# Output stage of a two-branch decoder layer on one core: zero fill, weight sums and merged sums moved between engines and places, last store moved from one queue to another

## What is computed

```python
h = rmsnorm(x, norm_g)
proj = einsum('bsd,dc->bsc', h, w_in)          # 1024 x 6656, then split
# branch A: three groups of 4 heads, (window, dilation) = (128,1), (512,4), (2048,16)
y_a = einsum('bsc,cd->bsd', attn_a * silu(z_a), w_pa)
# branch B: 8 heads, blocks of 256 keys; with 512 positions every query sees all its past
y_b = einsum('bsc,cd->bsd', attn_b * silu(z_b), w_pb)
merged = sigmoid(r_a + b_a) * y_a + sigmoid(r_b + b_b) * y_b
x = x + einsum('bsd,de->bse', merged, w_out)
out = rmsnorm(x, final_g)
```

## Time and profile before

| what | value |
|---|---|
| median of 3 runs | 436.65 us (433.98 to 437.82) |
| the profiled execution's own time | 436.65 us |
| its span, first to last instruction | 434.8 us |
| around the span | 1.85 us |
| PE busy | 423.1 us, 97% of the span |
| DVE, ACT, POOL busy | 299.6, 228.3, 218.6 us |
| mean granted clock of PE | 0.992 |

### The profile page before, as it was taken

How to read it: one execution, slowest core, us unless ns; L and a number is a source line. 1 busy time by engine, 2 the same in 40 slices (tenths; PEclk the granted TensorE clock), 3 DMA queues, 4 the chain that set the end, 5 groups by cost and what they waited for, 6 DMA issues and landing times.

```text
span 434.8 us, 7147 instructions
## 1 busy us (share of the span) xinstructions
PE 423.1 (97%) x2557; PEld 376.6 (87%) x2557; DVE 299.6 (69%) x512; ACT 228.3 (53%) x475; POOL 218.6 (50%) x155
## 2 busy tenths in 40 slices
PE   6999999999999999999999999999999999999994
PEld 5789998889889888998888888888999999988883
DVE  3869835265577695766857675495687768589955
ACT  6645555355465676466654565354445544532633
POOL 4854433243274563585559545353435443734890
PEclk9899999999999999999999999999999999999998
DMA  8972244926899879431530217530442144199905
GB/s 286 291 197 99 98 112 132 290 73 243 312 271 338 340 266 296 155 99 28 167 96 0 99 45 283 193 103 31 134 134 77 65 129 133 38 387 405 408 9 194
DMA packets 48835, 76.70 MB, mean 176 GB/s; under 512 B 4360, under 2 KB 39200, under 8 KB 47264
## 3 DMA queue, kind: packets, MB, share of 16 engines
q1 hardware_dynamic: 43904, 67.38, 47.1%
q10 hardware_dynamic: 4896, 8.86, 5.6%
HBM read 55.21 MB, written 14.73 MB: 161 GB/s over the span
## 4 chain that ended last, share of the span: by engine, by line
PE 87%; DMA 6%; DVE 2%; ACT 2%; issue 1%; SPq 0%; DVEq 0%; ACTq 0%
PE ps L1102 14%; PE ps L1103 14%; PE ps L1106 14%; PE ps L1302 5%; PE ps L1301 5%; PE ps L1300 5%; PE ps L1143 4%; PE ps L1145 4%; PE ps L1144 4%; PE ps L1209 3%; PE ps L1190 3%; PE ps L1349 3%; PE ps L1348 3%; PE ps L1347 2%; PE ps L1228 2%; PE ps L1238 2%
## 5 line engine op out<-in xcount | busy, mean ns | idle before, releaser
L925 POOL TENSOR_TENSOR w_lo<-raw,w_hi 128x1024 fp32r<-128x1024 f32 x39 | 96.5, 2474 | 106.0 <-ACT w_hi L1401 105.9
L1102 PE MATMUL ps<-hT_hi,w_hi 128*128 128x512 f32 x240 | 97.7, 407 | 0.3 <-DVE hT_lo L1800 0.3
L1106 PE MATMUL ps<-hT_lo,w_hi 128*128 128x512 f32 x240 | 93.8, 391 | 0.0
L1103 PE MATMUL ps<-hT_hi,w_lo 128*128 128x512 f32 x240 | 93.8, 391 | 0.0
L994 POOL TENSOR_TENSOR w_lo<-raw,w_hi 128x512 fp32r<-128x512 f32 (+1 forms) x34 | 42.5, 1268 | 49.5 <-ACT w_hi L1423 49.5
L1106 PEld LDWEIGHTS ps<-hT_lo,w_hi 128*128 128x128 f32 x240 | 45.1, 188 | 9.9
L1102 PEld LDWEIGHTS ps<-hT_hi,w_hi 128*128 128x128 f32 x240 | 45.2, 188 | 6.8 <-issue 0.7
L1103 PEld LDWEIGHTS ps<-hT_hi,w_lo 128*128 128x128 f32 x240 | 45.3, 189 | 6.1
L1143 PE MATMUL ps<-w_hi,hT_hi 128*128 128x256 f32 x160 | 45.5, 285 | 0.0
L1145 PE MATMUL ps<-w_lo,hT_hi 128*128 128x256 f32 x160 | 44.7, 279 | 0.0
L1144 PE MATMUL ps<-w_hi,hT_lo 128*128 128x256 f32 x160 | 44.6, 279 | 0.0
(11 more groups left out here) (258 smaller groups left out, 1039.9 us busy)
## 6 DMA issues: line engine op xcount, KB each, us to landing
raw<-in_w_in SPq DMA_DIRECT2D x25, 1024.0 KB, 6.1
output_weight_sums<-ws_parts ACTq DMA_DIRECT2D x12, 512.0 KB, 4.4
KTs<-KTs SPq DMA_DIRECT2D x20, 256.0 KB, 4.4
folds<-folded_early SPq DMA_DIRECT2D x4, 1024.0 KB, 8.8
wq_raw<-in_w_out SPq DMA_DIRECT2D x4, 1024.0 KB, 11.3
folded<-folds SPq DMA_DIRECT2D x4, 1024.0 KB, 6.4
t_three<-output_weight_sums SPq DMA_DIRECT2D x2, 2048.0 KB, 11.8
raw<-in_w_out SPq DMA_DIRECT2D x3, 1024.0 KB, 5.0
```

Source lines behind the costliest of these rows:

```text
L925: nc.gpsimd.tensor_tensor(ring(w_lo, n, kt), src, ring(w_hi, n, kt).bitcast(F32), ALU.subtract).then_inc(lo_ready, 1)
L1102: pe.matmul(out, wh, hh, start=(k == 0), stop=False)
L1103: pe.matmul(out, wl, hh, start=False, stop=False)
L1106: return pe.matmul(out, wh, hl, start=False, stop=(k == kts - 1))
```

## The change

The zero block is written by DVE at the end of slot 22 instead of by POOL, and its semaphore goes. The last weight sum moves from the beginning of slot 22 to its end, and its low part to the end of slot 23. In the operations, `merged_sum(2, 1)` moves behind the merge of block 6, and ACT's casts of sum 2 by one operation. ACT's casts of `wo` 2 and 3 move behind the loop over the operations, so behind the cast of block 7. Sums 0 and 1 and their four low parts all come ahead of both additions that take product 7 out. The second half of tile 0 is stored by SP in its turn, not by ACT.

```diff
-W_PLACES = [(13, 1), (14, 1), (15, 1), (16, 0), (16, 1), (17, 0), (17, 1), (18, 1), (19, 1), (20, 1), (21, 1), (22, 0)]
-W_END = (22, 1)
+W_PLACES = [(13, 1), (14, 1), (15, 1), (16, 0), (16, 1), (17, 0), (17, 1), (18, 1), (19, 1), (20, 1), (21, 1), (22, 1)]
+W_END = (23, 1)
-ZERO_SLOT = 23
+ZERO_SLOT = 22
@@ SP
             for i in (2, 3, 0, 1):
                 for e in range(2):
-                    if i == 0 and e:
-                        continue
@@ POOL
-                if n - 2 == ZERO_SLOT:
-                    pool.wait_ge(ws_ready, 9)
-                    pool.wait_ge(third_ready, 3)
-                    for t in (pT_hi, pT_lo):
-                        nc.gpsimd.tensor_scalar(t[:, T_ZERO:T_ZERO + P], ident[:], 0.0, None,
-                                                ALU.mult).then_inc(zeros_ready, 1)
@@ PE, values
-                    if h.n == NDIL * HU:
-                        pe.wait_ge(zeros_ready, 2)
@@ ACT
-                if o == R_DONE + 2:
+                if o == R_DONE + 3:
                     for c in range(2):
                         ms_high(2, c)
-                if o == R_DONE + 5:
-                    for m in (2, 3):
-                        split_high(("wo", m))
                 prepare(o)
+
+            for m in (2, 3):
+                split_high(("wo", m))
@@ ACT, its last instructions
-            act.wait_ge(scaled[0], 2)
-            act.dma_start(out_t[:, 0, 512:1024], u_seven[:, 0, :]).then_inc(stored, 16)
@@ DVE, slots
                 weight_sums((s, 1))
+                if s == ZERO_SLOT:
+                    dve.wait_ge(ws_ready, 9)
+                    dve.wait_ge(third_ready, 3)
+                    for t in (pT_hi, pT_lo):
+                        link(nc.vector.tensor_scalar(t[:, T_ZERO:T_ZERO + P], ident[:], 0.0, None, ALU.mult))
@@ DVE, operations
                 prepare(o)
-                if o == R_DONE + 1:
-                    for c in range(2):
-                        merged_sum(2, c)
+                if R_DONE < o <= R_DONE + 2:
+                    merged_sum(2, o - R_DONE - 1)
                 if o == R_DONE + 3:
                     for c in range(2):
                         merged_sum_low(2, c)
             merged_low(ND - 1)
+            for n in range(2):
+                for c in range(2):
+                    merged_sum(n, c)
+            for n in (1, 0):
+                for c in range(2):
+                    merged_sum_low(n, c)
...
-            for n in range(2):
-                for c in range(2):
-                    merged_sum(n, c)
-                src = scaled_product(7, n)
-                dve.wait_ge(one_ready, n + 1)
-                add_product(u_seven[:, n, :], src, u_one[:, n, :], seven_ready)
-            for n in (1, 0):
-                for c in range(2):
-                    merged_sum_low(n, c)
+            for t in range(2):
+                src = scaled_product(7, t)
+                dve.wait_ge(one_ready, t + 1)
+                add_product(u_seven[:, t, :], src, u_one[:, t, :], seven_ready)
```

More of the change, by code:

```diff
@@ L491, in hybrid_layer_program @@
         ws_out = [sem(f"ws_out{i}") for i in range(3)]
-        zeros_ready = sem("zeros_ready")
         third_ready = sem("third_ready")
```

## The result

The changed kernel takes **438.75 us** in the median of 20 runs (436.44 to 442.63), the kernel before 436.48 in 20 runs beside it (433.83 to 440.98). The ratio is 1.0064 with a 95% interval of 1.0038 to 1.0091, so the change costs 2.8 us, between 1.7 and 4.0. The profiled execution took 437.65 us with a span of 435.8, again 1.85 around the span.

What follows compares the result with a forecast made beforehand. PE, busy 97% of the span, was taken as the bound, so edits could only cost. Slots 1.1, product 6 1.5 and store 0 made 2.6 us on 436.65: 439.25 us, range 436.5 to 441.5.

Steps and rivals of the forecast that it cites:

- Zeros and the last sum: Slots 22 to 24: a zero instruction is held behind POOL's, and PE's third fill of scores waits for its mask; +1.1 us.
- rival of zeros that pass freely: Slots 22 to 24: DVE's zero instructions are not held up by POOL, +0.4 instead of +1.1, so 438.55 us; chance 0.15.
- Block 7 later by 1.83: Operations on DVE: block 7's low part starts 1.83 us later, with sum 2 behind block 6's merge; no cost by itself.
- Product 2 later by 1.0: Output products: POOL's low part of `wo` 3 ends near 401.9, so product 2 starts at about 401.95, 1.0 us late.
- Product 6 later by 1.5: Output products: DVE's additions end at 407.75, product 6 starts 1.5 us later; product 2's delay lies inside this.
- POOL keeps the port: At `merged_sum(0, 1)`: POOL's second part takes the shared port at once, DVE waits 2.35 us more, 441.6 us; chance 0.14.
- The covers hold: Start of product 6: both additions of product 7 end by 406.35, nothing there moves PE; 436.75 us with free zeros; chance 0.1.
- The store: End of kernel: SP issues the store, three stores stand in the same line for DMA engines; 0, between -0.3 and +0.4 us.
- The base: The profiled execution of the kernel before, 436.65 us, as the median, to which the forecast added its 2.6 us.

## Why the prediction was right

It said 439.25 us, +2.6, and the measurement is +2.8 (1.7 to 4.0). By its steps:

- **Zeros and the last sum, +1.1: measured +1.16.** The first zero instruction took 2.35 (forecast 2.2), the second 0.23. The step itself was late by 0.18 (forecast 0.1 to 0.2), and the third fill then waited 0.87 for the mask (forecast 0.9); 0.1 more lies in the wider spacing of the matmuls behind the wait, which I did not have. It was right for the reason given: rows from another place of the same trace, with the same shape and the same two engines, carried over. The rival of zeros that pass freely falls at this place; in the kernel with the sums put back they do pass, because they come first.
- **Block 7 later by 1.83: measured 1.64.** The merge began as forecast (+3.88 ahead of product 1, measured 3.83), and the row of instructions up to block 7's low part was 0.24 shorter than I had added up.
- **Product 2 later by 1.0: measured 0.75.** The mechanism was as forecast, with two terms somewhat large: POOL's pair ended at +11.52 where I had 401.9, which is +11.87. Block 7 gave 0.19 of that, and the waiting of DVE's second addition was 0.62 (1.32 instead of 0.70), not 0.75.
- **Product 6 later by 1.5: measured 1.25** (+16.32 to +17.57), by the same two terms. By the last matmul 0.12 comes to it that I did not have, since the first matmuls behind the wait are spaced wider.
- **POOL keeps the port: falls.** DVE got in between POOL's two instructions.
- **The covers hold: falls** for the changed kernel: the additions end at +17.42 and had to by +16.32. With sum 2 in one piece they end at +15.78, and it holds.
- **The store, 0: measured -0.13**, and the queue makes 0.01 of it. What the 0.13 is was not tried; in the kernel before one DVE instruction of the tail ran beside POOL's last pair and took 0.91 instead of 0.75.
- **The base.** I set the sum on a profiled execution of 436.65 because it was the median. It contained the stall of the earlier trace rows, which I noted as a wait and did not price; it is worth 1.7 and comes and goes. The forecast holds against the medians, not between the two profiled executions, whose spans differ by 1.0. It served as a base only because it stood at the median.

What I did not forecast is that the edits do not add: with ACT's casts alone undone product 6 started later than with the whole change, and the order of the additions is free as long as DVE is not late.

## What to carry to other kernels

Where one engine is busy 97% of the time, the price of an edit is its delay minus the cover of whoever waits, and covers are shared: two edits that each fit can fail together, and undoing one alone can make a wait longer. Before placing a short DVE instruction look at what POOL does at that very time; here it was free when it began 0.80 ahead of POOL's instruction (0.22), took 2.35 when it began 0.13 behind its start, and a source in PSUM avoided it (0.28). When two traces differ, align them at the last point that the change can't have touched and compare places, since a stall elsewhere can be as large as the effect.

## What the runs showed that was not expected

- An idle time of 1.85 us on PE was followed by about 3 us at the lower granted clock in one trace (0.50), while one of 1.81 us in another (near 144, in the kernel with the additions put back) was followed by this (same columns as above):

```profile
145.20:147.00 1.80, 1.69 (x10) 1.13 (x10) 0.31 (x1) 1.80 (x8) 0.79 (x1) 1.00 0.82 332
```

  What makes the difference stays open; the idle times of 0.2 to 0.8 never lowered it, nor did one of 1.12 (at 137, with the zeros from PSUM) and one of 1.34 (near 144, with the early `wo` casts).
- A stall costs PE more than its idle time: about 0.15 that the end of the matmul before it hides, and 0.12 of wider spacing behind each of the two waits of the output products. Near 144 it was 0.91 on top of 0.78, mostly because each of the four transposes waited for its own exponential, and the profile's list of waits showed only the first.
- When POOL has a second instruction ready, a waiting DVE instruction gets in between: DVE's 1.32 instead of 0.70. POOL's pair then took 5.48 instead of 4.76; its first half, begun during DVE's addition of two SBUF tiles (395.57 to 396.27), took 2.68, the second 2.83.
